# Chunk products that share a stationary matrix become one matmul of 128 columns, with the chunk layouts swapped for it

## The reference, cut to what matters

```python
def wkv7_scan(r, w, k, v, a_vec, b_vec):
    def step(state, inp):
        r_t, w_t, k_t, v_t, a_t, b_t = inp
        sa = jnp.einsum('bhvk,bhk->bhv', state, a_t)
        state = (state * w_t[:, :, None, :] + sa[..., None] * b_t[:, :, None, :]
                 + v_t[..., None] * k_t[:, :, None, :])
        return state, jnp.einsum('bhvk,bhk->bhv', state, r_t)
...
def rwkv7_mixer(...):
    ...
    a = jax.nn.sigmoid(a0 + a_lr @ a_up)
    kk = (k * k_k).reshape(B, S, H, d)
    kk = kk / jnp.maximum(jnp.sqrt(jnp.sum(jnp.square(kk), axis=-1, keepdims=True)), 1e-12)
    k = k * (1.0 + (a - 1.0) * k_a)
    ...
    y = wkv7_scan(rh, decay, kh, vh, -kk, kk * ah)
    y = head_group_norm(y, gn_w, gn_b, GN_EPS_RWKV)
    bonus = jnp.sum(rh * kh * r_k, axis=-1, keepdims=True) * vh
    return (y + bonus.reshape(B, S, W)) * g
```

## Time and profile before

| | |
|---|---|
| median of 3 runs | 1346.81 us (1343.62 to 1348.06) |
| the profiled execution, its time / its span | 1342.93 us / 1341.1 us |
| granted TensorE clock, mean | 0.986 |
| TensorE matmul busy, share of the span | 1268.3 us, 95% (8636 records) |
| VectorE / ScalarE / GpSimd busy | 713.4 (53%) / 545.9 (41%) / 543.5 (41%) us |
| last slab before the chunk stage ends | 252.3 us |
| chunk stage, to the start of the next slabs' norms | 252.3 to 376.2 us |

### The profile page before, as it was taken

One profiled execution on the slowest core, in us unless ns is written; L12 is line 12 of the kernel. 1 busy time (PEld: TensorE's weight loads), 2 busy tenths in 40 slices (PEclk: granted clock), 3 DMA queues, 4 the chain that ended last, 5 costly groups with the idle time before them and its releaser, 6 DMA issues.

```text
span 1341.1 us, 21433 instructions
## 1 busy us (share of the span) xinstructions
PE 1268.3 (95%) x8636; PEld 1007.8 (75%) x8636; DVE 713.4 (53%) x838; ACT 545.9 (41%) x734; POOL 543.5 (41%) x253
## 2 busy tenths in 40 slices
PE   6999999678799999999999999999999999999995
PEld 3777757467778877788888888888776777777873
DVE  7887756937548652246315234144477845442833
ACT  4332253253244343353223222134433458886342
POOL 4342222550137652265444444445534332223453
PEclk9999999899999999999999999999999999999998
DMA  6561111110034321032322223322422321111221
GB/s 225 156 219 63 63 63 47 48 34 4 5 127 155 113 79 63 32 110 88 101 95 94 95 96 100 103 95 94 149 80 87 102 87 58 68 65 63 95 94 63
DMA packets 35100, 119.94 MB, mean 89 GB/s; under 512 B 4544, under 2 KB 4672, under 8 KB 34624
## 3 DMA queue, kind: packets, MB, share of 16 engines
q1 hardware_dynamic: 29808, 105.78, 23.6%
q10 hardware_dynamic: 5200, 12.85, 3.1%
HBM read 111.01 MB, written 2.10 MB: 84 GB/s over the span
## 4 chain that ended last, share of the span: by engine, by line
PE 76%; DVE 15%; ACT 4%; issue 2%; DMA 1%; ACTq 1%; POOL 0%; DVEq 0%; SPq 0%
PE banks L1392 19%; PE banks L1394 19%; PE banks L1393 19%; DVE y_mid L847 2%; DVE tmp L847 1%; PE banks L1876 1%; PE banks L1413 1%; PE banks L1892 1%; PE banks L1414 1%; PE banks L1415 1%; DVE qk L847 1%; DVE kx L847 1%; PE banks L1981 1%; PE banks L1966 1%; DVE a_lo L855 1%
## 5 line engine op out<-in xcount | busy, mean ns | idle before, releaser
L330 POOL TENSOR_TENSOR w_lo<-w_raw,w_hi 128x1024 fp32r<-128x1024 f32 x145 | 354.7, 2447 | 537.2 <-ACT w_hi L410 537.2
L410 ACT ACTIVATE w_hi<-w_raw 128x1024 fp32r<-128x1024 f32 x145 | 153.8, 1061 | 336.8 <-PE banks L1394 217.4
L1392 PE MATMUL banks<-a_hi,w_hi 128*128 128x512 f32 x584 | 235.5, 403 | 14.2 <-DVE a_lo L855 12.4
L1394 PE MATMUL banks<-a_hi,w_lo 128*128 128x512 f32 x616 | 241.4, 392 | 0.0
L1393 PE MATMUL banks<-a_lo,w_hi 128*128 128x512 f32 x584 | 228.7, 392 | 0.0
L1394 PE MATMUL banks<-b_hi,w_lo 128*128 128x512 f32 x384 | 149.7, 390 | 0.0
L1392 PEld LDWEIGHTS banks<-a_hi,w_hi 128*128 128x128 f32 x584 | 110.2, 189 | 49.0 <-issue 16.9
L1394 PEld LDWEIGHTS banks<-a_hi,w_lo 128*128 128x128 f32 x616 | 116.2, 189 | 24.8
L847 DVE TENSOR_TENSOR x_res<-banks,x_res 128x512 f32<-128x512 f32 x56 | 38.7, 692 | 178.2 <-PE banks L1394 177.9
L330 POOL TENSOR_TENSOR w_lo<-w_raw,w_hi_mlp 128x1024 fp32r<-128x1024 f32 x36 | 87.2, 2423 | 106.6 <-ACT w_hi_mlp L410 106.6
L1393 PEld LDWEIGHTS banks<-a_lo,w_hi 128*128 128x128 f32 x584 | 110.5, 189 | 21.5 <-issue 0.7
(11 more groups left out here) (384 smaller groups left out, 2412.2 us busy)
## 6 DMA issues: line engine op xcount, KB each, us to landing
w_raw<-in_weights SPq DMA_DIRECT2D x189, 512.0 KB, 3.2
x_in<-in_x SPq DMA_DIRECT2D x4, 512.0 KB, 6.8
rot<-qk ACTq DMA_DIRECT2D x32, 64.0 KB, 2.0
decay<-in_decay ACTq DMA_DIRECT2D x1, 2048.0 KB, 9.0
x_res<-in_x ACTq DMA_DIRECT2D x4, 512.0 KB, 5.3
out_fm<-x_res SPq DMA_DIRECT2D x8, 256.0 KB, 2.1
consts<-in_consts SPq DMA_DIRECT2D x1, 1209.0 KB, 11.9
q_twice<-q_twice ACTq DMA_DIRECT2D x8, 128.0 KB, 3.1
```

What stands on the lines that cost most here:

```text
L330: nc.gpsimd.tensor_tensor(o, a, b, op).then_inc(S(name), 1)
L410: return nc.scalar.activation(o, a, f, **kw)
L1392: mm(o, high[:, w], hi[:, kc, :], start=kc == first, stop=False)
L1394: done = mm(o, w_lo[:, s % 4, w], hi[:, kc, :], start=False, stop=kc == last)
```

## The change

Products with the same stationary matrix are joined: ax against [kk | rx] (ABR), kx against [kk | rx] (AKR), each 128 columns wide, and in `transitions` the solved matrix against [RB | b_tok] (AT and QT). For this kk and rx lie side by side (`kr`), b in token-major form is stored beside AB and RB (ABR has three parts), and the two halves of the partitions now hold other chunks (chunk index t by half p and the turned layout are swapped). One mask of 128 columns, applied by VectorE, serves both parts, so ScalarE's copies of RB and RK and GpSimd's masks go, and so does `queries`. `tok` of a is no transpose any more but 32 matmuls against the identity, for its halves have to change places. `first_rhs` and `solve` now write to the other half of PSUM too. The order at the end is `chunk_states`, `transitions`, then the copies of QT.

In the preparation: the key factor is made by ScalarE right behind the sigmoid (k_mul), the key product by VectorE two slabs later; `ret_gate` stands in the chunk stage; the chunk decays are made once for all four tiles, ahead of the first mask. ScalarE waits for all four gates before it copies k in token-major form.

```diff
-        kx = at("kx", 152, [P, NF, T])
-        rx = at("rx", 160, [P, NF, T])
+        kr = at("kr", 152, [P, 2, NF, T])
+        kk, rx = kr[:, 0], kr[:, 1]
+        k_mul = at("k_mul", 102, [P, NF, T])
+        ABR = at("ABR", 78, [P, NF, 2, TT, 3, CH])
+        AKR = at("AKR", 102, [P, NF, 2, TT, 2, CH])
...
                         actv(ax[:, i, :], psum[4 + i % 2][:], sigmoid, bias=V("a0", i)).then_inc(A("lora_ready"), 1)
+                        if i == 0:
+                            act.wait_ge(S("s_ret_ready"), 4 * RH)
+                        actv(k_mul[:, i, :], ax[:, i, :], ACT.Identity, bias=one_ka[:, i:i + 1], scale=V("k_a", i)).then_inc(A("k_mul_ready"), 1)
...
+                    if kind == 2:
+                        for h in range(2):
+                            actv(ABR[:, :, h, t, 2, :], src.rearrange("p (f h e) -> p h f e", f=NF, h=2)[:, h], copy).then_inc(
+                                A("tok_ready" if h else "act_step"), 1)
+                    else:
+                        if n == 3 * TT:
+                            act.wait_ge(S("ret_gated"), NF)
...
             act.dma_start(mem_in[:], ins["mem"]).then_inc(S("mem_loaded"), 16)
-            products(RB, 0, "rb_done")
...
+            for n in range(4, 16):
                 tok(n)
...
             for f in range(NF):
-                act.wait_ge(S("qt_done"), 2 * (f // 2) + 2)
-                actv(QT[:, f, :].rearrange("p (t u c) -> p u t c", u=2, c=CH), chunks(pair(f // 2, f % 2)), copy).then_inc(A("r_copied"), 1)
+                act.wait_ge(S("at_ready"), f + 1)
+                actv(QT[:, f, :].rearrange("p (t u c) -> p u t c", u=2, c=CH), chunks(whole(f))[:, :, 0:2 * TT:2, :], copy).then_inc(A("r_copied"), 1)
...
                 tt(kk[:, f, :], kk[:, f, :], psum[6 + f % 2][:], ALU.mult).then_inc(D("dve_step"), 1)
-                step(ts(pt[:, 0, :], ax[:, f, :], V("k_a", f), one_ka[:, f:f + 1], ALU.mult, ALU.add))
                 step(tt(ax[:, f, :], ax[:, f, :], kk[:, f, :], ALU.mult))
-                step(tt(kx[:, f, :], kx[:, f, :], pt[:, 0, :], ALU.mult))
...
-                step(recip(sr[:, f, 0:NCH - 1], ...))
-                step(tt(sc[:, f, 0:NCH - 1], ...))
+            def chunk_decays():
...
-                for f in ((0, 1, 2) if s == S_PREP + 2 else (3,) if s == S_PREP + 3 else ()):
-                    ts(kk[:, f, :], kx[:, f, :], V("k_k", f), None, ALU.mult).then_inc(D("kk0_ready"), 1)
+                for f in ((0, 1) if s == S_PREP + 2 else (2, 3) if s == S_PREP + 3 else ()):
+                    dve.wait_ge(S("k_mul_ready"), f + 1)
+                    tt(kx[:, f, :], kk[:, f, :], k_mul[:, f, :], ALU.mult).then_inc(D("kk0_ready"), 1)
+                    ts(kk[:, f, :], kk[:, f, :], V("k_k", f), None, ALU.mult).then_inc(D("kk0_ready"), 1)
...
-                    if f >= 1:
-                        ret_gate(f - 1)
+            chunk_decays()
...
+            def take_abr(f):
+                dve.wait_ge(S("decayed"), 3 * (f + 1))
+                dve.wait_ge(S("abr_done"), f + 1)
+                tt(ABR[:, f, :, :, 0:2, :].rearrange("p h t k c -> p h t (k c)"),
+                   whole(f).rearrange("p h (t c) -> p h t c", t=TT), masks, ALU.mult).then_inc(D("abr_ready"), 1)
...
+            take_abr(0)
+            take_abr(1)
             take_n(0)
             take_n(1)
             bonus(NF - 1)
+            take_akr(0)
+            take_akr(1)
+            take_abr(2)
+            take_abr(3)
+            ret_gate(0)
             take_n(2)
             take_n(3)
+            ret_gate(1)
+            take_akr(2)
+            take_akr(3)
+            ret_gate(2)
+            ret_gate(3)
...
+                    for u in range(2):
+                        at0 = (2 * (t // 2) + u) * P + (t % 2) * CH
+                        last = mm(o[CH * u:CH * u + CH], src[:, f, at0:at0 + CH], C("ident"), start=True, stop=True)
...
+                                o = banks[CH * p:CH * p + CH, 2 * f + h, t * P:(t + 1) * P].rearrange("q (k c) -> q k c", k=2)
+                                last = mm(o, keys[b:b + HD, f, c], kr[b:b + HD, :, f, c], start=True, stop=True)
...
             def solve(f):
-                            last = mm(psum[2 * f + h][r, t * P:(t + 1) * P], XT[r, f, h, t, :], GH[r, 2 * f + h, t].rearrange("p k e -> p (k e)"), ...)
+                                r, m, n = slice(CH * u, CH * u + CH), 2 * tp + p, 2 * h + tp
+                                o = banks[CH * p:CH * p + CH, 2 * f + u, n * P:(n + 1) * P]
+                                last = mm(o, XT[r, f, h, m, :], GH[r, 2 * f + h, m].rearrange("p k e -> p (k e)"), start=True, stop=True)
...
+                            o = banks[HD * h:HD * h + HD, 2 * f + p, t * P:(t + 1) * P].rearrange("q (k c) -> q k c", k=2)
+                            last = mm(o, GH[r, 2 * f + h, t, 0, :], ABR[r, f, h, t, 1:3, :], start=True, stop=True)
+                last.then_inc(S("at_done"), 1)
...
-            products(0, ax, kk, True, "ab_done")
-            products(1, ax, kk, True, "ab_done")
+            products(0, ax, P, "abr_done")
+            products(1, ax, P, "abr_done")
...
+                chunk_states(f)
+            for f in range(NF):
+                pe.wait_ge(S("bc_ready"), f + 1)
                 transitions(f)
-            for g in range(2):
-                pe.wait_ge(S("bc_ready"), 2 * g + 2)
-                queries(2 * g)
-                queries(2 * g + 1).then_inc(S("qt_done"), 2)
+            pe.wait_ge(S("r_copied"), NF)
             y_inputs(0)
```

More of the change, by code:

```diff
@@ L540, in _ @@
                 if s == S_PREP + 6:
+                    act.wait_ge(S("kk0_ready"), 2 * NF)
                     exps(0)
@@ L574, in turned @@
                 actv(XT[:, f].rearrange("p h t c -> p (h t c)"), psum[f if n < NF else 2 * f][:], copy).then_inc(A("xt_ready"), 1)
-            def products(dst, f, name):
-                act.wait_ge(S(name), f + 1)
-                actv(dst[:, f], chunks(pair(f)), copy).then_inc(A("r_copied"), 1)
             tok(0)
@@ L587, in _ @@
             act.dma_start(mem_in[:], ins["mem"]).then_inc(S("mem_loaded"), 16)
-            products(RB, 0, "rb_done")
-            products(RB, 1, "rb_done")
-            products(RK, 0, "rk_mm_done")
-            products(RK, 1, "rk_mm_done")
-            for n in range(4, 8):
-                tok(n)
-            products(RB, 2, "rb_done")
-            products(RB, 3, "rb_done")
-            for n in range(8, 12):
-                tok(n)
-            products(RK, 2, "rk_mm_done")
-            products(RK, 3, "rk_mm_done")
-            for n in range(12, 16):
+            for n in range(4, 16):
                 tok(n)
@@ L961, in bonus @@
                 tt(bon[:, f, :], psum[6 + f % 2][:], vx[:, f, :], ALU.mult).then_inc(D("prep_ready"), 1)
-            mixed = [(low, 0), (low, 1), (low, 2)] + [(d, f) for d in (kx, rx, vx) for f in range(NF)]
+            mixed = [(low, 0), (low, 1), (low, 2)] + [(d, f) for d in (kk, rx, vx) for f in range(NF)]
             for s in range(S_MK):
@@ L1663, in chunk_states @@
                         for h in range(2):
-                            r, e = slice(CH * p, CH * p + CH), (2 * f + h) * HD
-                            mm(place(2 * f + p, h, t), b_tok[r, t, e:e + HD], GH[r, 2 * f + h, t, 1, :], start=True, stop=False)
+                            r = slice(CH * p, CH * p + CH)
+                            mm(place(2 * f + p, h, t), ABR[r, f, h, t, 2, :], GH[r, 2 * f + h, t, 1, :], start=True, stop=False)
                     for p in range(2):
@@ L1670, in chunk_states, with transitions @@
                 last.then_inc(S("bc_done"), 1)
-            def queries(f):
+            def transitions(f):
                 for t in range(TT):
@@ L1691, in y_inputs @@
                             r, e = slice(CH * p, CH * p + CH), (2 * f + h) * HD
-                            last = mm(place(4 + 2 * (f // 2) + p, h, t, f % 2), v_tok[r, t, e:e + HD], RK[r, f, h, t, :], start=False, stop=False)
+                            last = mm(place(4 + 2 * (f // 2) + p, h, t, f % 2), v_tok[r, t, e:e + HD], ak_tile(f, 1)[r, h, t, :], start=False, stop=False)
                 last.then_inc(S("y_in_done"), 1)
@@ L1754, in _ @@
                 tok(n)
-            for g in range(2):
-                pe.wait_ge(S("r_copied"), 7 + g)
-                first_rhs((2 * g, 2 * g + 1))
+            for f in range(NF):
+                if f % 2 == 0:
+                    pe.wait_ge(S("akr_ready"), 3 + f // 2)
+                first_rhs(f)
             for f in range(NF):
```

267 lines of the change are left out of this document (104 added, 163 removed).

## The result

| | before | after |
|---|---|---|
| median (range), us | 1345.5 (1343.62 to 1348.06), 4 runs | 1326.14 (1325.4 to 1326.74), 4 runs |
| profiled execution, time / span | 1342.93 / 1341.1 | 1326.74 / 1325.0 |
| mean granted clock | 0.986 | 0.987 |
| TensorE matmul records | 8636 | 8300 |

The ratio is 0.9853, with an interval of 0.9837 to 0.987: 19.4 us faster, where the forecast had 14.5. The two traces differ by 16.1 us, the two medians by 19.4. That difference of 3.3 us is half of what has to be explained.

The account below looks back on a forecast made before the run. The hole at 235 to 369 us was bound in turn by VectorE, ScalarE and instruction-block waits. Gains 11 + 0 + 4.5, less 1.0 for low clock, made 14.5: 1332.3 by the median; own range 1329 to 1336, wide 1326 to 1340.

Parts of the forecast that it names:

- Preparation: Up to the first mask: shorter VectorE lists per tile bring it to 259.6 from 269.8, 10.2 us earlier; key factor costs 0.
- Products to the first level: First mask to last XT copy: ends at 291, 11 us earlier than 302.0; ScalarE's k copies newly wait for the fourth gate.
- Levels: 302.0 to 340.6: same work, gain 0, bound +1.5; 1.0 us taken back for a longer low clock in the first level.
- last_xt to the first state step: 335.7 to 362.9: 27.2 us becomes 22.7, gain 4.5, bounds 3 and 6.5; y_inputs(0) newly waits for QT's copies.
- block price: Where small matmuls run back to back, 128 records take 3.7 us, nearer 3.9 in later blocks, however fast the array is.
- State loop: From the first state step at 363.33: keeps its 13.3 us.
- 3.9 under the median: Profiled execution of before, 1342.93, against its median of 1346.81; the same offset turned 1328.4 into 1332.3.
- more gain: Rival, 14%: full clock in the middle (14), 6.5 at the end, no fall in the first level; gain 20, 1327.
- 4% branch: Part of the 14% rival: block waits hidden because the next block arrives in time; gain 14.5 + 4.2 = 18.7, 1328.
- The middle gives back more: Rival, 17%: half clock to 275, slow gates, ScalarE held by the gate in the middle stretch; gain 9, 1338.
- slower: Rival, 3%: four array quarters don't overlap at 128 columns, 107 ns a record; 15 us later, 1362.
- no difference: Rival, 4%: 54 ns a record, two quarters at a time, and table loads cost 2; gain 3, 1343.5.

Follow-up runs that it names:

- a_gates_idle: Changed kernel with gates 0 and 1 moved behind tiles 1 and 2, gates 2 and 3 behind the mask ABR(3); 1324.26 us, ratio 0.9829.
- a_trans_half: Changed kernel with transitions multiplying only the b_tok part, 64 columns instead of 128, so part of the output is missing; 1325.58 us, ratio 0.9849.
- a_trans_split: Changed kernel with each 128-column matmul in transitions split into two of 64, 128 more matmul records; 1328.31 us, ratio 0.9877.
- a_warm: Changed kernel plus 6 filler matmuls of 512 columns, results unread, in TensorE's three waits (first mask, XT, QT); 1322.37 us, ratio 0.9816.
- b_look2: Kernel before, unchanged, one more profiled execution to see where a long execution is long; 1345.77 us.
- b_look3: Kernel before, unchanged, another profiled execution for the same question; 1345.37 us.
- a_prod_split: Changed kernel with each 128-column matmul of ABR and AKR split into two of 64, 256 more matmul records; 1330.46 us, ratio 0.9894.

## Why the prediction came out as it did

- *Preparation.* First mask forecast at 259.6, measured 259.62, with every step of the last list within 0.1 us of its forecast. The key factor costs next to nothing: the work behind the last slab's matmuls starts at 252.31, and the page counts 48 table loads in both kernels. Right.
- *Products to the first level.* Forecast 291, measured 290.29: 11.7 gained instead of 11. The new wait came as described (3.13 us, released by the gate; copies at 282.10). a_gates_idle says that it costs 1.9 us of the time, 3.1 at the end of the state loop.
- *Levels.* One microsecond was taken back for a longer low clock; last_xt starts 34.4 us behind XT against 33.7 before, so 0.7 was lost. The low clock came as described (0.52 in 288.5 to 295.3), but 0.7 is less than what varies: in the five traces of before this stretch takes 32.7 to 34.8 us.
- *last_xt to the first state step.* Forecast 22.7, measured 23.1 (324.7 to 347.8). The block price held, and a_trans_half and a_trans_split bear it out: what transitions cost is 128 records. Here too the five traces of before differ, 25.8 to 27.3 us. solve's records on four quarters took 29 ns (3.67 us / 126), between the 27 taken and 36.
- *State loop.* Taken as unchanged at 13.3 us; it took 12.3. In before two issue waits stand in it:
```profile
366.73 0.28 PE L1692 MATMUL banks<-RK,v_tok 64*64 64x64 f32 x3 [1.33 <-issue]
370.46 0.28 PE L1692 MATMUL banks<-RK,v_tok 64*64 64x64 f32 x3 [1.40 <-issue]
```
In after none does, though TensorE ran at half clock for the first 5.6 us. The half clock is not why: from the first state step to VectorE's first instruction behind the loop it is 11.7 us in after (12.6 in before), 10.7 in a_gates_idle and 10.2 in a_warm, both at full clock, with issue waits of 0.31 and 0.56 in the one and 0.33 in the other. So the change took away more than the 1.0, and the half clock took a part back. Why the waits went is not shown; TensorE stands still for 1.41 and 0.94 us just before the loop. Missed by 1.0.

On the trace the sum is thus 14.5 against 16.1 us, and every stage stands within 1.0. That close a match is in part luck, since another execution of before would have moved single stages by 1 to 2 us. The premise that a microsecond won in the chunk stage is won at the end held here (16.0 at the end of the loop, 16.1 in the span), but not always: a_warm and a_gates_idle lost 1.4 and 1.3 us again behind it. **The step that failed is the last one**, from the trace to the median: "3.9 under the median", carried over as a constant. It was no constant. Of the 6.2 us between 1332.3 and 1326.14, 1.6 are the terms of the sum (0.7 + 0.3 − 0.4 + 1.0), 1.3 that the median of before was 1345.5 with one run more, and 3.3 that the profiled execution of before was a short one (2.6 under that median) and the profiled one of the changed kernel a long one (0.6 over). b_look2 and b_look3 show what the prediction couldn't read in its rows: in typical executions of before one issue wait is 2.1 us longer and ends 3 us later. In the changed kernel the block comes late too, but the wait is 0.34 us. That the traced execution of after is 0.6 over its median comes from four executions (1325.4 to 1326.74), and no cause is shown for it. From the trace alone the prediction said 1328.4, 1.7 from the profiled 1326.74. The 3.9 us, more than the spread that the sum claimed for most of its terms, should have been a question (what varies between executions, and does the change touch it?) and a term with ends 0 and 3.9.

The rivals: "more gain" gave nearly the right time, 1327, for other reasons. The clock did fall, in three stretches, and the part behind last_xt gave 4.1 us, not 6.5. Its 4% branch, the rule of the Trainium skill ("Runtime: NRT & Kernel Launch", "Instruction fetch mechanics") that crossing a block is mostly hidden, is contradicted here by the issue waits of 1.50 and 1.51 us after the change and by a_trans_half. "The middle gives back more" didn't come: half clock ended at 264.6, not 275, and the gates took 0.69 to 1.01 us. The four quarters overlap at 128 columns, so "slower" and "no difference" fall.

## What to carry to other kernels

Where small matmuls run back to back and issue waits stand between them, count the instructions, not the columns: in transitions, undoing the join of two products with a common stationary matrix cost 2.9 us on TensorE's timeline, and halving the columns gave nothing. Before a sum made on one trace is moved to the median, ask why that execution is off it; a wait that varies from one execution to the next can be made short by a change that wasn't aimed at it. Where fillers keep the clock up in one stage, look behind it for where it falls instead. Small elementwise work that nobody waits for belongs where its engine idles, but in front of a row of copies it holds all of them.

## What the runs showed of the hardware

- The block of 128 records with their weight loads that crosses transitions took 4.00 us at 64 columns (a_trans_half, 339.41 to 343.41) and 4.00 at 128 (after, 339.65 to 343.65).
- An instruction block can come late beside a 1 MB load. In eight of the fourteen traces its packets start within 0.4 us of the end of the load (280.31 and 280.34 in b_look2, 270.69 and 270.70 in after). The issue wait was then 3.48 and 3.43 us in b_look2 and b_look3, 2.05 in a_prod_split and 0.34 in after; in before, where the packets start 0.6 us into the load, it was 1.33.
- Low clock costs more than I expected in a stage where VectorE and ScalarE hold the chain too: six matmuls of filling gave back 3.8 us. They also moved one low stretch to behind the stage (0.54 in 379.6 to 383).
- One kernel had executions 9 us apart on one chip (spans of 1338.8 to 1347.7).
- Records of 128 columns with half the identity as weights (`tok` of a) took 59 ns each (57 in 3.38 us, 269.41), twice solve's 29.
